# A two-layer decoder trunk on one core: both PEER layers gathered in one uninterrupted stream, with the attention layer run behind it

## The reference

```
def _peer(xn, wq, subkeys, u, v):                  # per 128 tokens
    q = (xc @ wq).reshape(T, 8, 2, 128)
    s = einsum('thpd,pkd->thpk', q, subkeys)       # 2 x 128 keys per head
    s_top, i_top = top_k(s, 16)
    best_s, pos = top_k(all 256 sums of pairs, 16) # 16 experts per head
    gate = softmax(best_s)
    act = gelu(einsum('thkd,td->thk', u[idx], xc)) # 128 dot products of a token with rows of u
    return einsum('thk,thkd->td', gate * act, v[idx])
```

## Time and profile before

| what | value |
|---|---|
| time, median of 3 runs | 1925.04 us (1923.3 to 1927.89) |
| the profiled execution | 1929.11 us, its span 1927.3 us |
| gathering of layer 0 / layer 1 (first gather to last matmul) | 691.0 / 680.6 us |
| mLSTM and the vectors ahead of it | 215 us |
| setup of layer 0 / layer 1 | 49.5 / 49.6 us |
| `fox` | 233.1 us |
| busy share: PE, DVE, POOL, ACT | 80%, 58%, 52%, 19% |

### The profile page before, as it was taken

How to read it: one execution, slowest core, us unless ns; L and a number is a source line. 1 busy time by engine, 2 the same in 40 slices (tenths; PEclk the granted TensorE clock), 3 DMA queues, 4 the chain that set the end, 5 groups by cost and what they waited for, 6 DMA issues and landing times. The chain is left out here.

```text
span 1927.3 us, 15072 instructions
## 1 busy us (share of the span) xinstructions
PE 1547.9 (80%) x4756; PEld 768.6 (40%) x4756; DVE 1108.9 (58%) x2496; ACT 366.6 (19%) x859; POOL 1006.0 (52%) x1088
## 2 busy tenths in 40 slices
PE   2999797799877777777787887977887777777777
PEld 2646582224322222222276866842232222222222
DVE  4524366746676675744256753476576766757442
ACT  0112012111211111111142431121112111111111
POOL 1101037765777777777200000277777777777772
PEclk9996898999999999999998968989999999999999
DMA  6963579999999999999664702699999999999996
GB/s 248 403 267 99 188 259 407 409 407 409 408 409 409 409 409 410 409 409 410 240 225 175 278 7 96 213 408 409 409 409 409 409 409 409 409 410 409 409 410 237
DMA packets 193650, 653.66 MB, mean 339 GB/s; under 512 B 20354, under 2 KB 21028, under 8 KB 190500
## 3 DMA queue, kind: packets, MB, share of 16 engines
q0 software_dynamic: 152064, 562.10, 73.7%
q1 hardware_dynamic: 40976, 89.47, 12.9%
q10 hardware_dynamic: 532, 1.13, 0.2%
HBM read 651.58 MB, written 1.05 MB: 339 GB/s over the span
## 5 line engine op out<-in xcount | busy, mean ns | idle before, releaser
L1403 PE MATMUL pair<-peer_v,peer_diag 128*128 128x512 f32 x2048 | 1002.4, 619 | 265.3 <-DMA peer_v<-in_peer_v,peer_idx 251.8
L1577 DVE SCALAR_TENSOR_TENSOR peer_u<-peer_u,pair 128x1024 f32<-128x1024 f32 x512 | 623.7, 1219 | 452.1 <-DMA peer_u<-in_peer_u,peer_idx 452.0
L1403 PEld LDWEIGHTS pair<-peer_v,peer_diag 128*128 128x128 f32 x2048 | 356.4, 191 | 906.9 <-DMA peer_v<-in_peer_v,peer_idx 601.9
L1326 POOL DMA_INDIRECT peer_u<-in_peer_u,peer_idx x512 | 483.5, 944 | 277.1 <-issue 110.7
L1326 POOL DMA_INDIRECT peer_v<-in_peer_v,peer_idx x512 | 486.6, 950 | 181.2 <-issue 135.8
L1459 ACT ACTIVATE peer_diag<-ident,peer_w 128x128 f32<-128x128 f32 x512 | 170.5, 392 | 561.8 <-DVE peer_w L1557 416.1
L404 PE MATMUL pair<-peer_xnT,peer_wst 128*128 128x256 f32 x512 | 113.0, 379 | 2.8 <-DVE peer_xnT L311 2.8
L404 PEld LDWEIGHTS pair<-peer_xnT,peer_wst 128*128 128x128 f32 x512 | 96.2, 190 | 15.9 <-DVE peer_xnT L311 3.4
L1452 ACT ACTIVATE peer_act<-peer_dot 128x8 f32<-128x8 f32 x64 | 13.3, 208 | 432.1 <-DVE peer_u L1577 432.1
L408 PE MATMUL pair<-ml_wst,ml_xnT 128*128 128x512 f32 x192 | 84.8, 604 | 0.9 <-ACT ml_xnT L746 0.9
L472 PE MATMUL pair<-fx_w_hi,fx_xhl 128*128 128x256 f32 x384 | 74.0, 293 | 0.0
(11 more groups left out here) (255 smaller groups left out, 1169.0 us busy)
## 6 DMA issues: line engine op xcount, KB each, us to landing
ml_ada_w<-in_ada_w POOLq DMA_DIRECT2D x16, 1024.0 KB, 8.2
peer_wst<-in_peer_wq SPq DMA_DIRECT2D x8, 2048.0 KB, 10.5
ml_wst<-in_a_w_in SPq DMA_DIRECT2D x6, 2048.0 KB, 20.3
fx_ada_w<-in_ada_w SPq DMA_DIRECT2D x24, 512.0 KB, 5.2
ada_ada_w<-in_ada_w SPq DMA_DIRECT2D x8, 1024.0 KB, 7.3
ml_ada_w<-in_ada_w POOLq DMA_DIRECT2D x16, 512.0 KB, 3.9
peer_wst<-in_kv_ada_w SPq DMA_DIRECT2D x4, 2048.0 KB, 19.9
peer_u<-in_peer_u,peer_idx POOLq DMA_INDIRECT x512, 16.1
```

What stands on the lines that cost most here:

```text
L1326: eng.indirect_dma_start(slot[:, :], None, rows, bass.IndirectOffsetOnAxis(ap=idx[:, i, k:k + 1], axis=0)).then_inc(landed, 16)
L1403: mm = eng.matmul(acc[g][:, cols], diag[n % DIAGS][:, :], vb[n % V_SLOTS][:, cols], start=(k == 0), stop=(k == SEL - 1))
L1577: eng.scalar_tensor_tensor(out=u, in0=u, scalar=1.0, in1=x_tok[g][:, :], op0=ALU.mult, op1=ALU.mult, accum_out=dot[:, n:n + 1]).then_inc(d ...
```

## The change

`peer`, `fox` and `store` become one phase `trunk`. Its gathering runs over N = 512 tiles in four groups q of 128: layer 0 tokens 0-127 (q = 0), layer 0 tokens 128-255 (q = 1), and the same of layer 1 (q = 2, 3). The remaining work of layers 0 and 1 is written as generators, one per engine, whose pieces carry the tile at which they are due (`Behind`): `vectors` (12 weight blocks of 2 MB, one every 8 tiles from tile 16), and `chain(0)` and `chain(1)`, started at tiles 128 and 256. `chain(g)` finishes layer 0's PEER for group g, runs all of FoX and the query projection of layer 1 for these 128 tokens, and uses 14 weight blocks of 2 MB, so the weights of FoX and of layer 1's queries are loaded twice. All of these projections are plain float32 (`part`: 8 matmuls of 512 columns); the split product is gone. Weight slots go from 3 to 2, v slots from 10 to 9; diagonals and u slots stay at 8. `x_tok` lies in SBUF. In groups 1 and 2 every third tile's v rows are added by DVE into `vacc` in SBUF in place of the diagonal and the matmuls.

```
+    V_SLOTS = 9          # was 10; U_SLOTS = 8 and LAG = 12 stay
+    ACT_SHIFT, DVE_SHIFT, POOL_SHIFT = 5, 14, 14 + U_SLOTS
+    EVERY = 3
+    def on_dve(n):
+        return EVERY > 0 and SEL <= n < 3 * SEL and n % EVERY == 1 and 0 < n % SEL < SEL - 1
...
+        blocks = [(a["peer_wq"][0], n * WCOLS, WCOLS, True) for n in range(4)]
+        blocks += [(a["kv_ada_w"], n * WCOLS, WCOLS, VECTOR) for n in range(4)]
+        blocks += [(a["ada_w"][1], G1 * D + n * WCOLS, WCOLS, VECTOR) for n in range(8)]
+        for _ in range(G):
+            blocks += [(w, n * WCOLS, WCOLS, GROUP) for w, first in ((wk, 0), (wq, 0), (wk, 2), (wq, 2), (wo, 0))
+                       for n in range(first, first + 2)]
+            blocks += [(a["peer_wq"][1], n * WCOLS, WCOLS, GROUP) for n in range(4)]
+        pj = Project(ph, blocks, slots=2)
...
+        x_tok = [ph.sb(f"x_tok{g}", [P, D]) for g in range(G)]
+        ROW_AT, VEC_AT, VEC_EVERY = 8, 16, 8
+        START = [SEL * (g + 1) for g in range(G)]
+        END = [39, 46]
+        WQ_EVERY = 3
...
+class Behind:
+    def upto(self, at):
+        while self.at is not None and self.at <= at:
+            tile = next(self.pieces, "end")
+            self.at = None if tile == "end" else at + 1 if tile is None else tile + self.shift
...
         # POOL
+            behind = Behind(roots(), POOL_SHIFT)
             for n in range(N + LAG):
...
+                    behind.upto(n)
                     gather(u_rows, n, ub[n % U_SLOTS], u_in[n % U_SLOTS])
...
+                    if m >= V_SLOTS and on_dve(m - V_SLOTS):
+                        eng.wait_ge(added, dve_before[m - V_SLOTS] + 1)
+                    elif m >= V_SLOTS:
+                        eng.wait_ge(summed, pe_before[m - V_SLOTS] + 1)
...
         # PE, the projections of chain(g); s = START[g], e = s + END[g]
+                yield s + 8        # K, units 0 and 1 at s+8, s+10; Q at s+12, s+14
+                yield from project(U_K, bank[4], B)
...
+                yield s + 18       # V at s+18, s+20; O at s+24, s+26
+                yield from project(U_V, bank[4], B)
...
+                yield e + 2        # output at e+2, e+4; queries at e+13, +16, +19, +22
+                yield from project(U_OUT, bank[6], B)
...
         # DVE
+            def add_v(m):
+                eng.wait_ge(v_in[m % V_SLOTS], 16 * (m // V_SLOTS + 1))
+                eng.wait_ge(w_done, m // BATCH + 1)
...
+                    eng.scalar_tensor_tensor(out=vacc[:, :], in0=vb[m % V_SLOTS][:, :], scalar=w[:, m:m + 1],
+                                             in1=vacc[:, :], op0=ALU.mult, op1=ALU.add).then_inc(added, 1)
...
+            for n in range(N):
...
+                eng.scalar_tensor_tensor(out=u, in0=u, scalar=1.0, in1=x_tok[q % G][:, :], op0=ALU.mult,
+                                         op1=ALU.mult, accum_out=dot[:, n:n + 1]).then_inc(dot_done, 1)
...
+                ahead.upto(n)      # routes: i = 1..7 from tile 14, 8..11 from tile 201, 12..15 from tile 336
...
+                if n >= DVE_SHIFT and on_dve(n - DVE_SHIFT):
+                    add_v(n - DVE_SHIFT)
+                behind.upto(n)     # vectors, then chain(0) and chain(1), 14 tiles after their number
...
 def program(nc, a, out):
-        mixers = (mlstm, fox)
-        for layer, mixer in enumerate(mixers):
-            mixer(nc, chip, a)
-            peer(nc, chip, a, layer)
-        store(nc, chip, out)
+        mlstm(nc, chip, a)
+        trunk(nc, chip, a, out)
```

More of the change, by code:

```diff
@@ L382, in load, with part @@
         for b, (w, col, width, fm) in enumerate(self.blocks):
-            if b >= self.SLOTS:
-                eng.wait_ge(self.done, self.last[b - self.SLOTS])
+            if b >= self.n_slots:
+                eng.wait_ge(self.done, self.last[b - self.n_slots])
             rows = "(p c) n -> p c n" if fm == VECTOR else "(c p) n -> p c n"
-            eng.dma_start(self.slots[b % self.SLOTS][:, :, 0:width],
+            eng.dma_start(self.slots[b % self.n_slots][:, :, 0:width],
                           w.rearrange(rows, p=P)[:, :, col:col + width]
-                          ).then_inc(self.loaded[b % self.SLOTS], 16)
+                          ).then_inc(self.loaded[b % self.n_slots], 16)
+    def part(self, eng, u, out, xT, first, count):
+        b, _ = self.units[u]
+        w = self.slots[b % self.n_slots]
+        if first == 0:
+            eng.wait_ge(self.loaded[b % self.n_slots], 16 * (b // self.n_slots + 1))
+        for c in range(first, first + count):
+            mm = eng.matmul(out[:, :], xT[:, c * P:(c + 1) * P], w[:, c, :], start=(c == 0), stop=(c == DC - 1))
+        if first + count == DC:
+            mm.then_inc(self.done, 1)
     def unit(self, eng, u, out, xT):
@@ L1318, in _ @@
             pj.load(eng)
+            for g in range(G):
+                eng.wait_ge(x_ffn, G + g + 1)
+                eng.dma_start(out[g * P:(g + 1) * P, :], x[:, g, :]).then_inc(stored, 16)
+            eng.wait_ge(stored, 16 * G)
         @block.gpsimd
@@ new lines, in everything @@
+            def everything():
+                yield from vectors()
+                yield from chain(0)
+                yield from chain(1)
+            eng.wait_ge(copied, G)
+            behind = Behind(everything(), 0)
+            for n in range(N):
+                q, k = divmod(n, SEL)
+                if not on_dve(n):
+                    eng.wait_ge(v_in[n % V_SLOTS], 16 * (n // V_SLOTS + 1))
+                    eng.wait_ge(diag_done, pe_before[n] + 1)
+                    if k == 0 and q >= 2:
+                        eng.wait_ge(x_ffn, q - 1)
+                    for half in range(2):
+                        cols = slice(half * 512, (half + 1) * 512)
+                        mm = eng.matmul(acc[q % 2][:, cols], diag[pe_before[n] % DIAGS][:, :], vb[n % V_SLOTS][:, cols],
+                                        start=(k == 0), stop=(k == SEL - 1))
+                    mm.then_inc(summed, 1)
+                behind.upto(n)
@@ L1447, in _, with vectors @@
                     take_s(u - 1)
+                if u in (2, 3):
+                    eng.wait_ge(tok_turned, u - 1)
+                    eng.activation(x_tok[u - 2][:, :], pair[0][:, :], ACT.Copy).then_inc(copied, 1)
             exponent(0)
+            def vectors():
+                yield ROW_AT + 1
+                rows.act(eng, 0, row_ffn, pair[2])
+                for u in range(VECTORS):
+                    yield VEC_AT + VEC_EVERY * u + 1
+                    eng.wait_ge(pj.done, VEC + u + 1)
+                    if u >= 2:
+                        eng.wait_ge(vec_ps, u - 1)
+                    eng.activation(row[0:1, (u % 2) * WCOLS:(u % 2 + 1) * WCOLS], bank[4 + u % 2][0:1, :], ACT.Copy
+                                   ).then_inc(row_done, 1)
+                yield VEC_END + 6
+                rows.act(eng, 1, row_mix, pair[2])
@@ L1449, in _, with everything @@
+            def everything():
+                yield from vectors()
+                yield from chain(0)
+                yield from chain(1)
+            behind = Behind(everything(), ACT_SHIFT)
             for b in range(N // BATCH):
@@ L1597, in _ @@
-            weigh(N // BATCH - 1)
-            add_residual(1)
-def store(nc, chip, out):
-    with ExitStack() as ctx:
-        stored = ctx.enter_context(nc.semaphore("stored"))
-        block = ctx.enter_context(nc.Block())
-        @block.sync
-        def _(eng):
-            for g in range(G):
-                eng.dma_start(out[g * P:(g + 1) * P, :], chip.x[:, g, :]).then_inc(stored, 16)
-            eng.wait_ge(stored, 16 * G)
+            ahead = Behind(routes(), DVE_SHIFT)
+            behind = Behind(everything(), DVE_SHIFT)
```

1225 lines of the change are left out of this document (660 added, 565 removed).

## The result

The changed kernel takes 1904.55 us (1894.5 to 1907.67, 4 runs) against 1926.05 us (1923.3 to 1927.89, 4 runs) of the kernel before in the same comparison: ratio 0.9881, interval [0.984, 0.9921]. It is 1.2% faster, clear of the interval and in the direction that was forecast, but 58 us slower than the forecast of 1847 and above its range (1815 to 1885, and 1805 to 1895 for 8 in 10). The gain is 21.5 us where 78 were forecast. The profiled execution took 1907.06 us, its span 1905.3.

What follows compares the result with a forecast made beforehand. DMA at 409 GB/s was taken to bound the gathering, with POOL only 3% behind. A floor of 1807 us plus 10 for the chains and 30 for dots blocking POOL gave 1847 us; range 1815 to 1885, 8 in 10 within 1805 to 1895.

Steps and rivals of the forecast that it cites:

- Stages, bytes, DMA's 409 GB/s: Whole gathering: FoX stage and second setup go, 83.9 MB of weights join the gathers; 620.8 MB at 409 GB/s, 1517.8 us.
- the floor: Whole kernel with DMA as bound and nothing lost to port or chains: 1807 us; as a rival 1807 to 1815, chance 17%.
- Setup, start and tail: Outside the steady gathering: 264.5 + 1.5 us up to the first gather, 17.6 start and tail, 8 at the end.
- PE under DMA: Chains' dense stretches: PE 96 us against DMA's 105, then 84 against 97; without tiles on DVE, 110 in the first.
- DVE's time: Where routes, additions and chain pieces meet: DVE needs 2.45 us a tile, under DMA's 2.56, so the added work is free.
- The dot on POOL: Tiles without weight loads: two-SBUF-input dots block POOL's gathers; 2 + 28 = 30 us at 2.78 a tile, bounds 0 to 98.
- B: Rival: POOL becomes the bound outside weight loads, reads falling at random; 1915 us, with half of it 1866; beyond 1885 12%.
- D: Rival: slower than before, POOL's lock in all groups, 3.19 us a tile in the middle ones; 1971 us, chance 6%.
- The formula for reads at random: Gathers hitting dots at random: 3.04 us a tile, 0.48 over DMA; 3.19 in the middle groups with additions.
- Chains: Both chains: waits on two weight slots and between engines, 5 us each, 10 in all; bounds 0 to 84.
- 22 tiles late: Four rsqrt on POOL per chain come 22 tiles late, behind what they wait for, so cost nothing.
- C: Rival: chains stall on two weight slots loading in series; 1891 us, or near 1900 with half the POOL blocking; chance 13%.

Runs made afterwards that it cites:

- e4: Changed kernel with dot and DVE addition both replaced by sums over one SBUF tile, products and additions left out: 1838.99 us, ratio 0.9548.
- e1: Changed kernel with no v tile added by DVE, all going through the diagonal and PE: 1877.16 us, ratio 0.9731.
- e3: Changed kernel with the DVE addition replaced by a sum over the v tile, dots keeping two SBUF inputs: 1879.48 us, ratio 0.9758.

## Why the prediction was wrong, step by step

**Stages, bytes, DMA's 409 GB/s: right.** One gathering of 1628 us stands in place of two; where nothing stalls it runs at 409, and 0 of the last 107 tiles' 274 us are lost. The kernel without its two-input dots and additions (`e4`) takes 1839 us, 32 above the floor of 1807.

**Setup, start and tail: right.** The trunk's setup is 50.1 us where 51.0 was reckoned; it began at 219.9 in this execution against 215.0, so that the first gather starts at 270.0, 4 us later than forecast. In the experiments at 409 GB/s it starts between 264.3 and 269.6, in most of them at 265 to 266, as forecast. The end took 7.3 for 8.

**PE under DMA: right.** Taking DVE's third away (`e1`) made the kernel faster. With all tiles on PE the first part of chain 0 takes 97 us as before, that of chain 1 164 in place of 160. But "moving them is worth its cover" was wrong: the additions cost 27 us.

**DVE's time: right and of no matter.** The dot takes 1.225 us where 1.28 was reckoned, the addition 1.276; with the same time and one input the two together cost 65 us less.

**The dot on POOL: the step that failed.** The mechanism was right (nearly every long gather ends 0.81 us behind a dot or an addition, mean 1.11 us), the term of the sum was too small: 30 us forecast, 65 measured (`e4` against the changed kernel), inside its bounds of 0 to 98. Two things are missing in it.

First, the additions. The prediction works T = 2.78 out with the 1.28 us of the dot alone. It has the additions as time of DVE ("free") and as relief for PE ("worth its cover"), and as holders of the port only in rivals B and D. In the sum they stand at nothing; they cost 25 us on top of the dots (`e3` against the changed kernel). A tile among routes takes 3.15 us with them and 2.81 without (tiles 384 to 404), and the second is close to the 2.78 of the forecast.

Second, the stretches with weight loads, where "a tile has 3.2 us and POOL has room" and nothing was counted. The columns `e3` and `e4` of the table differ by the dots' edit alone. Their difference is 43 us, of which 13 are lost up to tile 196 and in tiles 262 to 330, beside weights.

The remaining 30 us of that difference equal the 2 + 28 forecast for the tiles without weights, in part by luck. The forecast spreads 28 us evenly over the last 190 tiles; 20 came in the 74 tiles of 330 to 404, 1 in the last 107, and in 196 to 262 it was 9 where 2 were forecast. "The dots are so regular in the row" was read off, and that stretch is like the last 107 tiles, not like those among routes.

The formula for reads at random looks better than it is. It gives 3.04 us a tile, and `e1` has 223/74 = 3.01 in tiles 330 to 404; with additions it gives 3.19, and the changed kernel has 237/74 = 3.20. But `e1`'s gathers there have a mean of 1.11 us, so that they and their gaps of 0.30 make 2.83 us a tile, and the changed kernel's 1.22, which makes 3.05. The rest is time in which POOL waits for PE to free a v slot (some 23 and 18 us in all beyond the usual gaps). Without the additions, blocked reads were fewer than at random. What these waits for PE cost by themselves was not tested; `e4` has waits of the same kind there and loses 1.5 us.

**Chains: undersized.** 10 us forecast; `e4`, whose gathers are hardly blocked, ends 32 us over the floor, and the table has 17.0 of these in the two first parts of the chains and 4 in the second ones. The wait on weights is the kind that I weighed: 9.4 us in chain 0 and 4.1 in chain 1 in the changed kernel, 8.7 and 9.1 in `e4`. The other kind I priced at nothing: the rsqrt on POOL. The one at the head of chain 1 comes 16 us after its mean and PE waits 15.9 us for it. "22 tiles late" counts POOL's own tiles, and POOL was 13 gathers short of its tile when the mean was ready. How much of the 21 us is the rsqrt's, and whether a third slot helps, is not settled.

**The rivals.** B comes nearest: POOL sets the pace among routes, and 1904.55 lies between its half (1866) and its full size (1915). The mechanism is B's, the number partly luck, since its 98 us hold no additions, count all of the last 190 tiles and have no chain beyond 10. Its part beyond 1885 had 12%. C's series of loads did not come: PE waited for weights 9.4 us at the longest. (C with B's half is 1807 + 84 + 49 = 1940, not 1900, and D's 266 + 1587 + 60 + 18 + 8 is 1939, not 1930.) D's price of a tile with additions, 3.19, is near the 3.15 of tiles 384 to 404, but such tiles are some 140 of the 256 that it took for them, and its 3.1 on average was not reached.

**The signs named ahead.** The mean of the gathers, their ends 0.81 us behind a dot and the pace over 3 us (in tiles 384 to 404 of the last group) came as said for B. DMA slices below 380 GB/s at the chains, named as C's sign, came too (down to 322), but it does not tell B and C apart: the chains' first parts run at 364 and 370 GB/s in the changed kernel and at 379 and 382 in `e4`, with no series of loads in either. DMA was not at 409 in the dense stretches, as it should have been by the forecast.

The sum after, against 1847: 35 more for the dots and additions, some 17 for the chains and what else is left, 4 for the later start, 1 or 2 for the median. This splits the 58 with rounded parts; the 17 are the remainder, and port and chains overlap.

## What to carry to other kernels

If two engines share a port, list every instruction that will hold it, also those that were added to relieve a third engine, and put the time of all of them into one sum. An instruction that is free by its engine's busy time can still cost on the other engine: here DVE had the time for the additions, and they cost 25 us.

Then ask of each stretch whether anything disturbs the two engines' phase. In step they cost nothing; out of step a tile took 2.81 us with the dot alone and 3.15 with additions, against 2.56, and they can stay out of step for 30 tiles after the disturbance has ended. Moving an operand from PSUM to SBUF is not free when GpSimd issues indirect gathers. A tiny instruction that a chain needs does not belong in the queue of the engine that sets the pace.
